# First mixer: query norm folded into the angles, the transposed copies and the exponent; the keys' rotary part turned once; its 64 columns made as rows; other banks and another order of work

## The chip, the cores and the metric

The kernel runs on one core of one Trainium2 chip. The metric is the device time of one execution in microseconds (us); the median of three runs before the change is 1462.47 us (1462.24 to 1466.19). Engines: TensorE (PE: matmuls; PEld: its weight loads), VectorE (DVE), ScalarE (ACT), GpSimd (POOL), and SyncE (SP), which issues the DMAs.

## The reference, cut to what matters

Two transformer blocks on 256 tokens of width 1024, in float32. The change lies in the first block's mixer, mainly in its latent attention:

```python
c_q, c_kv, k_r, hq, hf_f, hf_b, hi, hg = split(rms_norm(x, g_mix) @ w_in)
q  = (rms_norm(c_q,  g_qa)  @ w_qb).reshape(.., 4 heads, 192)      # 128 plain + 64 rotary columns
kv = (rms_norm(c_kv, g_kva) @ w_kvb).reshape(.., 4 heads, 256)     # 128 for k, 128 for v
k  = concat([k_nope, k_r for every head])                          # 128 + 64 shared
q, k = rms_norm(q, g_qn), rms_norm(k, g_kn)                        # over the 192 columns
q, k = [plain part, rope(rotary part, cos, sin)]                   # x1*cos - x2*sin, x1*sin + x2*cos
a  = softmax(q @ k.T * 192**-0.5) @ v
r  = hgrn2(hq, hf_f, hf_b, hi, hg)      # gated linear attention, both directions, chunks of 64
x  = x + concat([a, r]) @ w_o
```

Then a gated feed-forward part, an embedding part (`w_ple_gate`, `w_ple_proj`), and the second block.

## The kernel before

Weights come in 441 units of 128x1024 float32 in the order of a list (`plan`). SP issues unit u's DMA into one of four `raw` buffers once unit u-4 was split. ACT makes the upper half `wh` (`high(n)`: up to unit n), after PE is done with unit u-4; DVE makes the rest `wl` (`low(n)`), and PE waits for it (semaphore `lo`). Each product is three matmuls (upper x upper, upper x lower, lower x upper) into one of eight PSUM banks. `hTh`/`hTl` are the turned, normalised input in two halves, `lTh`/`lTl` the turned latents, `mh`/`ml` the turned mixer output.

Every engine runs one instruction stream in the order in which its function is written, and stops at each `wait_ge`. That hand-written order is what sets the schedule. The unit kinds: `unit_T` gives tokens as rows (two halves q of 128 tokens), `unit_E` gives columns as rows (128 columns by 256 tokens), `unit_D` is a rank-128 update of a 256x1024 sum.

The first mixer's stages on PE: `w_in` 0 to 511 (latents, units 0 to 3); unit 4, the 64 rotary key columns (48 matmuls that move 64 columns each); the forward gates (`gate(0)` to `gate(3)`, `unit_E`) with the latents' transposes behind `gate(1)`; `w_qb` and `w_kvb` (units 9 to 12); `q_part(0..3)`; `heads_turned` (transposes of the plain parts of q or k and of the rotated parts `qr`); the value units (`w_in` 2112), with the keys' `heads_turned` inside; `gate(4)`; `score(0)`, `score(1)`, `inner`, and so on; `hg(0..3)` (`w_in` 2624); the output projection `w_o(0..3)` between the chunk states (`states`) and their outputs (`output`), then its units 4 to 7 by halves; `w_ple_proj`; the feed-forward loop.

On DVE, query and key heads go the same way (lines 708 to 734): mean of squares, root on POOL (`root`, an ALU.pow on 8 columns), eight scalings by root and gain (L717), and the turning by angle (L731, L732, L734), all ahead of PE's transposes. `kr` (the 64 columns) is copied from PSUM at L609 and repeated into `kf` at L611. ACT copies the transposes into `qTn`, `kTn`, `qTr` (L1425); `vt` is copied behind `to_end(0)` (L1541). POOL multiplies the forward `qz` (L443).

## Time and profile before

| | us |
|---|---|
| median of 3 runs | 1462.47 |
| the profiled execution | 1460.53 |
| its span, first to last instruction | 1458.8 |
| PE busy | 1414.6 (97%) |
| DVE busy | 970.9 (67%) |
| ACT busy | 791.7 (54%) |
| POOL busy | 43.2 (3%) |
| mean granted PE clock | 0.990 of full |

The span is cut by instruction spans on each engine; 1.7 us of the execution lie around it. Matmuls overlap in the record, so PE's work is best read from one start to the next. "[idle before <-releaser]" behind a row tells how long the engine stood idle before it and which engine, tile and line ended that.

### The profile page before, as it was taken

How to read it: one execution, taken by the hardware profiler on the slowest of the kernel's cores; microseconds unless marked ns; L12 is line 12 of the kernel's file. 1: busy time of each engine (PE TensorE's matmuls, PEld its weight loads, DVE VectorE, ACT ScalarE, POOL GpSimd, SP SyncE). 2: the span in 40 equal slices, each digit the busy share in tenths (PEclk: the TensorE clock that was granted, in tenths of full speed). 3: DMA queues.
4: the chain of work that ended last, by engine and by line, in shares of the span. 5: the costliest groups of instructions: out<-in, count | busy, mean ns of one | idle time of the engine just before them, and what ended most of it. 6: DMA issues, size and time to landing. Idle time of an engine off the chain costs nothing.

```text
span 1458.8 us, 23164 instructions
## 1 busy us (share of the span) xinstructions
PE 1414.6 (97%) x9070; PEld 1280.6 (88%) x9070; DVE 970.9 (67%) x1738; ACT 791.7 (54%) x1468; POOL 43.2 (3%) x48
## 2 busy tenths in 40 slices
PE   7989999999999999999999999999999999999996
PEld 6878799999787787799999999999998888888885
DVE  6767655555764565768999577778865555555554
ACT  6856444444553554455445677777745455454552
POOL 2211200000000000000000000000000000000000
PEclk9999999999998999999999999999999999999999
DMA  7423365555442345555555544444455656655552
GB/s 251 145 89 136 102 222 185 184 188 179 158 145 98 110 139 171 190 188 170 179 172 165 184 145 144 133 143 146 137 168 189 242 189 194 195 190 199 189 195 79
DMA packets 66925, 241.66 MB, mean 166 GB/s; under 512 B 8192, under 2 KB 8576, under 8 KB 66432
## 3 DMA queue, kind: packets, MB, share of 16 engines
q1 hardware_dynamic: 66816, 240.17, 50.4%
q8 instruction: 73, 1.20, 0.3%
q14 instruction: 36, 0.29, 0.1%
HBM read 238.04 MB, written 2.10 MB: 165 GB/s over the span
## 4 chain that ended last, share of the span: by engine, by line
PE 85%; DVE 10%; ACT 3%; issue 1%; DMA 0%; POOL 0%; SPq 0%; DVEq 0%; POOLq 0%; ACTq 0%
PE bank L2000 83%; DVE wl L523 3%; PE bank L2075 1%; ACT wh L1419 1%; DVE eq L1289 1%; DVE eq L1292 1%; DVE ij L1295 1%; PE bank L2063 1%; DMA x<-in_x 0%; POOL st L439 0%; DVE t L660 0%; DVE e L666 0%; DVE e L669 0%; DVE pos__220 L1226 0%; DVE h L541 0%
## 5 line engine op out<-in xcount | busy, mean ns | idle before, releaser
L523 DVE TENSOR_TENSOR wl<-raw,wh 128x1024 fp32r<-128x1024 f32 x429 | 523.7, 1223 | 292.6 <-ACT wh L1419 292.1
L1419 ACT ACTIVATE wh<-raw 128x1024 fp32r<-128x1024 f32 x429 | 451.2, 1055 | 259.4 <-PE bank L2000 256.9
L2000 PE MATMUL bank<-hTh,wh 128*128 128x256 f32 x1632 | 471.0, 289 | 8.9 <-ACT vt L1425 5.1
L2000 PE MATMUL bank<-hTh,wl 128*128 128x256 f32 x1632 | 464.2, 284 | 0.0
L2000 PE MATMUL bank<-hTl,wh 128*128 128x256 f32 x1632 | 464.0, 284 | 0.0
L2000 PEld LDWEIGHTS bank<-hTh,wh 128*128 128x128 f32 x1632 | 315.6, 193 | 11.8 <-ACT vt L1425 5.5
L2000 PEld LDWEIGHTS bank<-hTl,wh 128*128 128x128 f32 x1632 | 315.5, 193 | 0.8
L2000 PEld LDWEIGHTS bank<-hTh,wl 128*128 128x128 f32 x1632 | 315.0, 193 | 0.0
L2000 PE MATMUL bank<-wh,hTh 128*128 128x512 f32 (+1 forms) x760 | 253.8, 395 | 1.1 <-DVE hTl L549 0.7
L2000 PE MATMUL bank<-wh,hTl 128*128 128x512 f32 (+1 forms) x760 | 249.8, 389 | 0.0
L2000 PE MATMUL bank<-wl,hTh 128*128 128x512 f32 (+1 forms) x760 | 249.7, 389 | 0.0
L2000 PEld LDWEIGHTS bank<-wh,hTh 128*128 128x128 f32 x760 | 143.4, 189 | 31.0 <-issue 1.8
L2000 PEld LDWEIGHTS bank<-wh,hTl 128*128 128x128 f32 x760 | 143.6, 189 | 30.0
L2000 PEld LDWEIGHTS bank<-wl,hTh 128*128 128x128 f32 x760 | 143.9, 189 | 28.5
L1926 ACT ACTIVATE gates<-bank 128x256 f32<-128x256 f32 (+31 forms) x118 | 38.2, 324 | 77.1 <-PE bank L2000 77.1
L2000 PE MATMUL bank<-oi,oj 128*128 128x128 f32 x512 | 67.4, 274 | 0.0
L2000 PEld LDWEIGHTS bank<-oi,oj 128*128 128x128 f32 x512 | 62.7, 192 | 0.0
L1378 DVE TENSOR_TENSOR gates<-bank,gates 128x220 f32<-128x220 f32 (+31 forms) x64 | 32.9, 514 | 38.3 <-ACT gates L1425 38.3
L1924 ACT ACTIVATE ga<-bank 128x256 f32<-128x256 f32 (+32 forms) x73 | 21.0, 288 | 68.5 <-PE bank L2000 68.5
L439 POOL TENSOR_TENSOR st<-st,mhalf 128x1 f32<-128x1 f32 (+2 forms) x15 | 15.3, 1020 | 1333.0 <-DVE st L530 1126.6
L1383 DVE TENSOR_TENSOR hTl<-gates,hTh 128x256 fp32r<-128x256 f32 x126 | 52.5, 417 | 0.0
L1425 ACT ACTIVATE hTh<-gates 128x256 fp32r<-128x256 f32 x126 | 50.3, 400 | 0.0
(361 smaller groups left out, 1300.2 us busy)
## 6 DMA issues: line engine op xcount, KB each, us to landing
raw<-in_wts SPq DMA_DIRECT2D x441, 512.0 KB, 3.5
x<-in_x SPq DMA_DIRECT2D x2, 512.0 KB, 4.6
sk<-in_sk SPq DMA_DIRECT2D x1, 1024.0 KB, 6.4
spill<-x SPq DMA_DIRECT2D x1, 1024.0 KB, 7.9
x<-spill SPq DMA_DIRECT2D x1, 1024.0 KB, 5.6
out<-h SPq DMA_DIRECT2D x2, 512.0 KB, 2.6
gb<-in_g_mix SPq DMA_DIRECT2D x1, 512.0 KB, 4.6
gb<-in_g_ffn SPq DMA_DIRECT2D x1, 512.0 KB, 4.5
```

What stands on the lines that cost most here:

```text
L439: signal(e.tensor_tensor(o, ms, mhalf[:, 0:o.free_size()], ALU.pow), name)
L523: e.tensor_tensor(b[:, :], raw[u % RAW][:, :], a[:, :].bitcast(F), ALU.subtract).then_inc(S("lo"), 1)
L1289: n = own.up(e.tensor_tensor(eq[:, a, :, :, :], bc(paf[:, q, a, :, :], 3, 16), io, ALU.is_equal))
L1292: n = own.up(e.tensor_tensor(eq[:, a, :, :, :], eq[:, a, :, :, :], bc(f4[:, :, a, :], 2, 16), ALU.mult))
L1295: t = e.tensor_reduce(ij[:, a, q, :, :], eq[:, a, :, :, :], AX, ALU.add)
L1378: e.tensor_tensor(g, v[:, NE - 1 - n:NE, :], g, ALU.mult).then_inc(S("G"), 1)
L1383: e.tensor_tensor(b, gates[:, ORDER[n], :], a.bitcast(F), ALU.subtract).then_inc(S("al"), 1)
L1419: e.activation(parts_of(u)[0][:, :], raw[u % RAW][:, :], ACT.Copy).then_inc(S("hi"), 1)
L1425: return e.activation(o, i, ACT.Copy)
L1924: t = e.activation(ga[n % 5][:, 0:c], b[:, 0:c], ACT.Gelu)
L1926: t = e.activation(gates[:, ORDER[n], c:256], b[:, c:256], ACT.Gelu)
L2000: return e.matmul(o, l, r, start=first, stop=last, skip_group_check=True)
```

## The change

What it does, part by part:

- The query norm no longer scales `qf`. The gains of the plain part are applied as a per-partition scale in ACT's copy of the transposes (`gqk` is now 128x2, one column for q and one for k); the gains of the rotary part are multiplied into sine and cosine (`rot`, new DMA `gqkr`); the root itself scales the exponent of the softmax (`st[:, 32..39]`) and the negated maximum.
- The keys' rotary part is turned once (`keys_turned`, 128x64) and then multiplied by the four heads' roots (`kr4`); the plain part takes one 128x1024 product.
- Unit 4 is computed with its weights as the stationary operand (64 rows by 256 tokens), copied to `kt` and turned back by two transposes on PE.
- The first `w_kvb` unit uses banks 6 and 7, the second 2 and 3; the queries' transposes use banks 0 and 1 and stand between the `q_part` units.
- `score(0)`, `score(1)` stand ahead of `gate(4)`; ACT copies `vt` ahead of `to_end(0)`; the squares of the queries come after the copies of `kTn`.
- The forward `qz` product goes from POOL to DVE (`decayed_forward`), with its exponential kept in `hgs`. POOL's fills come earlier.
- `hg(3)` ahead of `inner(1,1)`; `w_o` units 0 to 3 by token halves, with the states' outputs and a transpose between the halves; `w_ple_proj`'s last unit by halves; DVE's and ACT's orders there.

```diff
@@ vector
             e.wait_ge(S("done"), nth("K", "w_in", 512, 64) + 1)
-            for q in range(2):
-                e.tensor_copy(kr[:, q, :], B[2 + q][:, 0:64]).then_inc(S("kr"), 1)
-            e.wait_ge(S("kr"), 2)
-            e.tensor_copy(kf[:, :, :, 128:192], bc(kr[:, :, :], 2, 4)).then_inc(S("kfr"), 1)
+            e.tensor_copy(kt[:, :], B[2][0:64, 0:256]).then_inc(S("krT"), 1)
...
             latent_low(1)
+            e.wait_ge(S("kr_ps"), 1)
+            e.tensor_copy(kr[:, :, :], B[3][:, 0:128].rearrange("p (q c) -> p q c", q=2)).then_inc(S("kr"), 1)
+            e.wait_ge(S("kr"), 1)
+            e.tensor_copy(kf[:, :, :, 128:192], bc(kr[:, :, :], 2, 4)).then_inc(S("kfr"), 1)
...
+            def keys_scaled(n):
+                k8 = kf[:, :, :, 0:128].rearrange("p q h c -> p (q h) c")
+                e.wait_ge(S("rs_1"), 2)
+                e.wait_ge(own.sem, n)
+                e.tensor_tensor(k8, k8, bc(st[:, 40:48], 2, 128), ALU.mult).then_inc(S("scaled"), 1)
+                e.tensor_tensor(kr4[:, :, :, :], bc(rk[:, :, :], 2, 4),
+                                bc(st[:, 40:48].rearrange("p (q h) -> p q h", q=2), 3, 64), ALU.mult).then_inc(S("rope"), 1)
...
             low(13)
+            n_rot = angles_weighted()
+            e.wait_ge(own.sem, n_rot)
+            n_rot = keys_turned()
             low(14)
             scan(0)
+            queries_turned()
             low(15)
             v_out(0)
             low(16)
             v_out(1)
-            headed(qf, 0)
             from_step(0, 31, "t1")
-            scaled(qf, 0)
-            headed(kf, 1)
+            headed(1)
             low(17)
-            turned_by_angle(qf, 0)
+            keys_scaled(n_rot)
             low(18)
-            scaled(kf, 1)
             low(19)
-            turned_by_angle(kf, 1)
             low(20)
             inner(0)
-            low(21)
             rope_out(0)
             rope_out(1)
+            headed(0)
+            low(21)
             from_step(0, 63, "t1b")
             low(22)
+            top_score(0)
+            top_score(1)
             low(23)
             k_decayed(0)
-            top_score(0)
-            top_score(1)
...
             low(25)
+            decayed_forward()
...
             out_mean(0)
+            out_scale(0)
             out_mean(1)
-            out_scale(0)
+            mixed_low(1, 0)
             low(35)
             out_scale(1)
-            mixed_low(1, 0)
@@ scalar
             q_out(0, 512)
+            q_out(1, 256)
+            high(14)
             logs(0)
-            high(14)
-            q_out(1, 256)
+            k_out(0)
             high(15)
-            k_out(0)
...
-            embedded(0)
             turn_high(1, 2)
             turn_high(1, 3)
+            embedded(0)
             embedded(1)
@@ tensor
+            def unit_K(unit, o):
+
+                wh_, wl_ = begin(unit)
+                for k in range(8):
+                    c = two(64, k)
+                    mm(o, wh_[:, c], hTh[:, k, :], k == 0, False)
+                    mm(o, wh_[:, c], hTl[:, k, :], False, False)
+                    t = mm(o, wl_[:, c], hTh[:, k, :], False, k == 7)
+                t.then_inc(S("done"), 1)
...
             gate(0)
+            e.wait_ge(S("krT"), 1)
+            for q in range(2):
+                p = e.transpose(B[3][:, two(64, q)], kt[:, two(128, q)], ident[0:64, 0:64])
+            p.then_inc(S("kr_ps"), 1)
             gate(1)
...
             e.wait_ge(S("t_lo"), 2)
+            unit_T(("T", "w_kvb", 0, 512, 0), B[6:8], lTh, lTl, 2, 512, True, True)
             e.wait_ge(S("qf"), 2)
-            unit_T(("T", "w_kvb", 0, 512, 0), B[2:4], lTh, lTl, 2, 512, True, True)
-            e.wait_ge(S("qf"), 4)
-            unit_T(("T", "w_kvb", 512, 512, 0), B[0:2], lTh, lTl, 2, 512, True, True)
-            for n in range(4):
-                q_part(n)
+            unit_T(("T", "w_kvb", 512, 512, 0), B[2:4], lTh, lTl, 2, 512, True, True)
+            q_part(0)
+            q_part(1)
             heads_turned(qf, 0, 0)
+            q_part(2)
             heads_turned(qf, 0, 1)
-            e.wait_ge(S("va"), 4)
+            q_part(3)
+            e.wait_ge(S("nope"), 2)
+            e.wait_ge(S("ropeT"), 2)
             for k in range(4):
                 unit_T(("T", "w_in", 2112, 512, k), B[0:2], hTh, hTl, 2 * k, 512, k == 0, k == 3)
-                if k == 2:
+                if k == 1:
                     heads_turned(kf, 1, 0)
                     heads_turned(kf, 1, 1)
-            gate(4)
             score(0)
             score(1)
+            gate(4)
             inner(0, 0)
```

Three places show how the rows move. First DVE, around the end of the 64-column unit (`kr` is its copy; `kt` and `krT` are new; `cq` the latents). Before:

```order
L605 COPY cq<-bank 128x512 x2
L523 TENSOR_TENSOR wl_63<-raw_55,wh_59 128x1024
L609 COPY kr<-bank 128x64 x2
L611 COPY kf<-kr 128x8x64
L530 TENSOR_SCALAR st<-st 128x4
L523 TENSOR_TENSOR wl_60<-raw_52,wh_56 128x1024
L618 SCALAR_TENSOR_TENSOR cq<-cq,st,gqa 128x256 x4
```

and DVE at the same place now:

```order
L605 COPY cq<-bank 128x512 x2
L523 TENSOR_TENSOR wl_63<-raw_55,wh_59 128x1024
L608 COPY kt<-bank 64x256
L530 TENSOR_SCALAR st<-st 128x4
L523 TENSOR_TENSOR wl_60<-raw_52,wh_56 128x1024
L615 SCALAR_TENSOR_TENSOR cq<-cq,st,gqa 128x256 x4
```

The two copies of `kr` and the one into `kf` went to behind the latents' lower halves; one copy of `kt` stands in their place, and PE now waits for it between `gate(0)` and `gate(1)`.

Second ACT, from the exponentials of `from_middle(0)` to the second direction's first gate (`vt` the values of the linear attention, `P` the softmax's exponentials). Before:

```order
L1533 ACTIVATE e_107<-t_105 128x1024
L1419 ACTIVATE wh_56<-raw_52 128x1024
L1419 ACTIVATE wh_57<-raw_53 128x1024
L1425 ACTIVATE kTn<-bank 128x4x128 x2
L1419 ACTIVATE wh_58<-raw_54 128x1024
L1541 ACTIVATE e_108<-t_105 128x1024
L1419 ACTIVATE wh_59<-raw_55 128x1024
L1425 ACTIVATE vt<-bank 128x512 x2
L1548 ACTIVATE P,sm<-bank,nm 128x256 x4
```

and ACT at the same place now:

```order
L1574 ACTIVATE e_108<-t_106 128x1024
L1458 ACTIVATE wh_56<-raw_52 128x1024
L1458 ACTIVATE wh_57<-raw_53 128x1024
L1458 ACTIVATE wh_58<-raw_54 128x1024
L1544 ACTIVATE kTn<-bank,gqk 128x4x128 x2
L1534 ACTIVATE sqm,st<-qf 128x192 x8
L1458 ACTIVATE wh_59<-raw_55 128x1024
L1464 ACTIVATE vt<-bank 128x512 x2
L1580 ACTIVATE e_109<-t_106 128x1024
L1587 ACTIVATE P,sm<-bank,nm,st 128x256 x4
```

The copy of `vt` passed the exponential L1541 (now L1580), and the eight squares of the queries came in behind `kTn`.

Third PE, from the last output of the linear attention (`St`, `qz`) to the first units of the second half of `w_o` (`o_` the normalised output, `mh_91` before and `mh_92` now the turned copy of it). Before:

```order
L2000 MATMUL bank<-vt,At 128x128
L2000 MATMUL bank<-St,qz 128x128
L2000 MATMUL bank<-wh_56,mh_90 128x512 x2
L2000 MATMUL bank<-wl_60,mh_90 128x512 x2
L2000 MATMUL bank<-wh_56,ml_92 128x512 x2
L2000 MATMUL bank<-wh_56,mh_90 128x512 x2
L2000 MATMUL bank<-wl_60,mh_90 128x512 x2
L2000 MATMUL bank<-wh_56,ml_92 128x512 x2
L2075 MATMUL bank<-ident,o__99 128x128 x4
L2000 MATMUL bank<-wh_57,mh_91 128x512 x2
```

and PE at the same place now:

```order
L2041 MATMUL bank<-St,qz 128x128
L2041 MATMUL bank<-wh_59,mh_91 128x512 x2
L2041 MATMUL bank<-wl_63,mh_91 128x512 x2
L2041 MATMUL bank<-wh_59,ml_93 128x512 x2
L2041 MATMUL bank<-wh_56,mh_91 128x512 x2
L2041 MATMUL bank<-wl_60,mh_91 128x512 x2
L2041 MATMUL bank<-wh_56,ml_93 128x512 x2
L2124 MATMUL bank<-ident,o__100 128x128 x4
L2041 MATMUL bank<-wh_56,mh_91 128x512 x2
L2041 MATMUL bank<-wl_60,mh_91 128x512 x2
L2041 MATMUL bank<-wh_56,ml_93 128x512 x2
L2041 MATMUL bank<-wh_57,mh_92 128x512 x2
```

The output stands half a unit earlier, and half a unit (three rows) now lies between the transposes of `o_` and the first product that reads them.

## Rows read from the trace of the kernel before

**Rows 1.** The page, part 1: busy time (share of the span) and instructions.

```profile
PE 1414.6 (97%) x9070; PEld 1280.6 (88%) x9070; DVE 970.9 (67%) x1738; ACT 791.7 (54%) x1468; POOL 43.2 (3%) x48
```

**Rows 2.** PE's waits from 0 to 260 us: in total, times, longest.

```profile
PE bank L2000 <- ACT vt L1425: 5.1, 1, 5.1
PE bank L2000 <- DVE ml L774: 2.0, 1, 2.0
PE bank L2122 <- DVE qr L734: 1.8, 1, 1.8
PE bank L2000 <- ACT hgs L1645: 1.1, 1, 1.1
PE bank L2000 <- DVE hTl L549: 1.1, 1, 1.1
PE bank L2000 <- ACT qf L1425: 0.8, 1, 0.8
```

**Rows 3.** Windows: us, then busy (x) of PE, PEld, DVE, ACT, POOL; PEclk, DMA share, GB/s.

```profile
12.31:23.53 11.22, 11.22 (x48) 9.04 (x49) 9.40 (x25) 7.46 (x10) 0.38 (x3) 1.00 0.72 232
23.53:28.81 5.28, 5.28 (x50) 5.28 (x48) 3.98 (x7) 2.49 (x10) 0.00 (x0) 1.00 0.66 206
28.81:36.15 7.34, 7.34 (x51) 7.34 (x51) 5.51 (x11) 4.40 (x5) 4.21 (x3) 0.77 0.60 191
36.94:42.76 5.82, 5.82 (x51) 5.82 (x49) 5.79 (x7) 3.10 (x6) 1.94 (x2) 1.00 0.54 177
42.76:54.65 11.89, 10.32 (x50) 8.21 (x49) 7.29 (x10) 8.68 (x13) 0.00 (x0) 1.00 0.53 162
60.00:80.00 20.00, 18.25 (x118) 16.35 (x117) 18.25 (x36) 17.88 (x40) 9.27 (x4) 1.00 0.34 119
87.00:91.38 4.38, 4.38 (x24) 4.38 (x25) 1.78 (x2) 0.36 (x1) 0.00 (x0) 0.62 0.60 226
```

**Rows 4.** DVE in order of time, 24 to 37 us: start, us, what [idle before].

```profile
29.70 1.23 DVE L523 TENSOR_TENSOR wl<-raw,wh 128x1024 fp32r<-128x1024 f32 x1 [2.12 <-ACT wh L1419]
30.84 0.35 DVE L609 COPY kr<-bank 128x64 f32<-128x64 f32 x2
...
33.77 1.67 DVE L618 SCALAR_TENSOR_TENSOR cq<-cq,st,gqa 128x256 f32<-128x256 f32 x4 [0.91 <-POOL st L439]
```

**Rows 5.** All engines in order of time, 83 to 88 us.

```profile
84.39 1.06 ACT L1541 ACTIVATE e<-t 128x1024 f32<-128x1024 f32 x1 [3.91 <-DVE t L660]
...
86.30 1.06 ACT L1425 ACTIVATE vt<-bank 128x512 f32<-128x512 f32 x2
...
86.93 0.58 PE L2000 MATMUL bank<-hTh,wh 128*128 128x256 f32 x1 [5.06 <-ACT vt L1425]
```

**Rows 6.** POOL in order of time, 30 to 130 us.

```profile
59.56 2.55 POOL L439 TENSOR_TENSOR st<-st,mhalf 128x8 f32<-128x8 f32 x1 [20.60 <-DVE st L530]
65.03 3.21 POOL L439 TENSOR_TENSOR st<-st,mhalf 128x8 f32<-128x8 f32 x1 [2.92 <-DVE st L530]
75.98 4.30 POOL L443 TENSOR_TENSOR qz<-e,qT 128x512 f32<-128x512 f32 x2 [7.74 <-DVE qr L734]
```

**Rows 7.** DVE's groups by line, 55 to 84 us: xcount | busy us, mean ns.

```profile
L666 DVE TENSOR_TENSOR e<-e,qT 128x1024 f32<-128x1024 f32 x1 | 2.3, 2314 | 0.0
```

**Rows 8.** DVE in order of time, 124 to 130 us.

```profile
126.84 1.23 DVE L666 TENSOR_TENSOR e<-e,qT 128x1024 f32<-128x1024 f32 x1 [0.80 <-ACT e L1532]
```

**Rows 9.** DVE in order of time, 106 to 111.5 us.

```profile
108.11 0.66 DVE L762 COPY PT<-bank 128x512 f32<-128x512 f32 x1
110.92 1.23 DVE L523 TENSOR_TENSOR wl<-raw,wh 128x1024 fp32r<-128x1024 f32 x1 [2.15 <-ACT wh L1419]
```

**Rows 10.** DVE in order of time, 146 to 160 us.

```profile
147.40 0.73 DVE L700 SCALAR_TENSOR_TENSOR St<-St,dl,bank 128x128 f32<-128x128 f32 x2
```

**Rows 11.** PE in order of time, 149 to 149.4 us.

```profile
149.26 0.38 PE L2000 MATMUL bank<-vt,At 128*128 128x128 f32 x2
```

**Rows 12.** ACT in order of time, 174 to 184 us.

```profile
180.31 3.92 ACT L1419 ACTIVATE wh<-raw 128x1024 fp32r<-128x1024 f32 x4
```

More of the change, by code:

```diff
@@ L1503, in nope_out @@
                 e.wait_ge(S("nope_ps"), 2 * i + q + 1)
-                copy((qTn, kTn)[i][:, :, 128 * q:128 * q + 128],
-                     B[(2, 6)[q]][:, :].rearrange("p (h t) -> p h t", h=4)).then_inc(S("nope"), 1)
+                e.wait_ge(S("in_small"), 112)
+                e.activation((qTn, kTn)[i][:, :, 128 * q:128 * q + 128],
+                             B[(2, 6)[q] if i else 0][:, :].rearrange("p (h t) -> p h t", h=4), ACT.Copy,
+                             scale=gqk[:, i:i + 1]).then_inc(S("nope"), 1)
             def rope_out(q):
@@ L1525, in decays @@
                              ACT.Exp).then_inc(S("dl"), 1)
[L1526 removed]
+                e.activation(e3b[:, :] if d else hgs[:, :, :].rearrange("p q c -> p (q c)"), b, ACT.Exp).then_inc(S("eb"), 1)
             def from_middle(d):
@@ new lines, in unit_K, with part_D @@
+            def unit_K(unit, o):
[6 more added lines that the diff above has]
+                t.then_inc(S("done"), 1)
+            def part_D(held, xh, xl, base, q, first, last):
+                s = two(128, q)
+                for a, b, f, z in ((xh, held[0], first, False), (xh, held[1], False, False), (xl, held[0], False, last)):
+                    for n in range(2):
+                        t = mm(B[base + 2 * q + n][:, :], a[:, s], b[:, two(512, n)], f, z)
+                return t
@@ L2048, in unit_D @@
             def unit_D(unit, xh, xl, base, first, last, half=False):
-                wh_, wl_ = begin(unit)
+                held = begin(unit)
                 for q in range(2):
-                    s = two(128, q)
-                    for a, b, f, z in ((xh, wh_, first, False), (xh, wl_, False, False), (xl, wh_, False, last)):
-                        for n in range(2):
-                            t = mm(B[base + 2 * q + n][:, :], a[:, s], b[:, two(512, n)], f, z)
+                    t = part_D(held, xh, xl, base, q, first, last)
```

251 lines of the change are left out of this document (139 added, 112 removed).

## The prediction

> **What bounds the kernel now.** I read the page's totals first. TensorE (PE) is busy 97% of a span of 1458.8 us [rows 1], so the end moves only if PE does less work, works at its higher clock for longer, or waits less. The change touches only the first block's mixer and the start of its feed-forward part, that is the first 183 us, so next comes who PE waits for there [rows 2]. The largest wait after the start is 5.1 us on a copy of `vt` by ScalarE (ACT). The others are 2.0 us on `ml`, 1.8 us on `qr`, 1.1 us each on `hgs` and `hTl`, and 0.8 us on the copy of `qf`. The windows then cut PE's row at the places that the change touches [rows 3]. They show two stretches where PE never idles and is slow all the same. From 28.81 to 36.15 the granted clock averages 0.77, and from 87.00 to 91.38 it averages 0.62: part of each runs at 1.2 GHz instead of 2.4. The first stretch follows the 5.28 us of the 64-column unit, the second follows the 5.1 us wait.
>
> **The change part by part.** Unit times are taken from start to start. One weight unit of 24 matmuls (128x256) at full clock takes 5.82/2 = 2.91 us [rows 3] (window 36.94:42.76).
>
> *The 64-column unit.* Before: 48 matmuls in 5.28 us, 110 ns each [rows 3]. After: 24 matmuls whose output is 64 rows by 256 columns. No row shows that form. The nearest is the 2.91 us unit, equal but for 128 output rows, and I take 2.9. The bounds are 24 x 110 ns = 2.6 us and 5.0 us, if the form ran at half clock. Gain 2.4 us.
> The trace shows 110 ns for a matmul that moves only 64 columns; a weight load of 128 columns stands beside each. The Trainium skill (TensorE: Matmul & The Clock Gate, "LDWEIGHTS (loading the stationary operand)") says that a weight load's time follows its columns, P/1.2 ns: about 107 ns for 128 columns and 53 for 64. By that page the new form is paced by its 256 moving columns, about 109 ns each (same page, "Back-to-back issue gap"), and the unit would be 2.6 us, 0.3 better than in my sum.
>
> *The clock behind it.* Two units ran in 7.34 us where 5.82 is full clock [rows 3]. With a full-rate moving operand in place of the 5.28 us of narrow matmuls I expect no drop there: gain 1.5. Bounds: 0 and 1.5.
>
> *The new wait.* `kr` used to be copied by VectorE (DVE) and nothing waited for it soon. Now PE, right behind `gate(0)`, must transpose `kt`, and DVE's copy of `kt` still stands behind the same `wl` (29.70) in DVE's queue, which itself waited for ACT [rows 4]. PE reaches the transposes at 23.53 + 2.9 + 2.91 = 29.3. The copy starts at 30.84 as before and takes 0.22 (one `kr` copy) to 0.42 (a 128x256 copy); I take 0.40, so it is done at 31.25. That is a wait of 1.9 us plus 0.25 for two transposes (bounds 0.1 and 0.6). Behind it `gate(1)` and everything on PE is queued. `gate(1)` ends at 34.4. The scaled latents then come 0.4 earlier than the row at 33.77, as DVE has less to copy; the fourth is ready at 35.1, so `latents(1)` adds 0.3. Loss 2.45 us. The first block up to w_qb thus gains only 2.4 + 1.5 - 2.45 = 1.45: it starts at 41.3 instead of 42.76.
>
> *w_qb and w_kvb.* 11.89 us with 10.32 busy [rows 3], so two gaps of 0.8 us. The first w_kvb unit goes to banks 6 and 7 and waits for no copy of `qf`, and the logarithm with its table load now stands behind both `q_out` on ACT. Both 0.8 us waits go; start to start this is 2.0 us, as the matmuls' overlap comes back too: 36 matmuls of 512 columns at 0.234 (11.22/48, window 12.31:23.53) and 12 of 256 at 0.121 make 9.9 against 11.89. Gain 2.0, bounds 1.5 and 2.1.
>
> *Queries and keys.* Queries now need no root, no scaling and no mean ahead of the rotation: `rope` is done when six DVE operations of 0.41 to 0.43 us follow the scan, at about 55, and PE asks for it at 57.7. The 1.8 us wait for `qr` goes: gain 1.75. What is late next is ACT's `nope`/`rope_out` of half 0, which PE asks for after `q_part(2)`, at 60.6. ACT's queue up to it (k_out, two `wh`, k_out, eight squares, a table load, `silu`, `wh`, `silu`, copies) sums to 60.4: 0.2 us spare. If it is late, PE pays that lateness one for one. A root of 8 columns on POOL took 2.55 and 3.21 us [rows 6]; with 3.2 the scaled keys are there at 65.0 and PE asks at 69.7. The queries' root is asked for only by the scores' maxima: done at 79.1, asked at 80.0.
>
> *DVE.* Sixteen scalings, two groups of 8 at 2.7 us each, become one 128x1024 product (1.2) and one 128x512 (0.7); the keys' six turning operations shrink to 128x64, with four small ones for the weighted angles. POOL no longer multiplies `qz` from 75.98 to 80.28 [rows 6], while DVE's product took 2.31 us [rows 7] against 1.23 for the same line with POOL idle [rows 8]: 2.2 us of DVE back for the two products. Added are two products for `qz`, 1.4 us, behind `low(25)`, ahead of the copy of `PT` at 108.11. They fit in the 2.15 us of idle that follows it [rows 9]; the copy ends at 110.2 where PE asked at 110.4. I take 0, bound 0.5 lost.
> The Trainium skill (GPSIMD Engine Reference, "Key points") says that GpSimd shares its SBUF interfaces with VectorE and contends with DVE instructions of two SBUF inputs. The 2.31 against 1.23 agrees.
>
> *The wait for vt.* Before, PE idled for 5.06 us up to 86.93 since ACT's copy of `vt` was queued behind an exponential that waited for DVE [rows 5]. After, the copy stands ahead of that exponential, and the scores stand ahead of `gate(4)`. By my walk PE ends the value units at 76.5; `kTn` and `kTr` are there by 74.2, `vt` at 77.2, and `gate(4)` wants it at 80.0. Gain 5.1, and with the idle goes the half clock behind it: 24 matmuls in 4.4 us at a granted 0.62 [rows 3] against 2.91, gain 1.5. Next late: the first probabilities, ready at 81.7, asked at 86.6. Bounds: 2 (if the root of the queries, behind eight squares, is the new end) and 6.6.
> The trace grants 0.62 right after that idle time. The Trainium skill (TensorE: Matmul & The Clock Gate, "What's actually happening") says that the half clock is the default and that activity releases it. By that page the new 1.9 us wait could bring half clock behind it, which would add 1.5 us to my sum; in the trace the 1.8 us wait for `qr` brought none (it lies in the window 60:80, with 1.00).
>
> *98.6 to 138.* Same work, shifted. Moving `hg(3)` ahead of `inner(1,1)` does not help: the 1.1 us wait for `hgs` ended on ACT's own queue. 0.
>
> *Output projection.* `output(1,*)` now starts half a `w_o` unit, 1.43 us, earlier than 149.26 (at 147.83), but needs the last `St`, done at 148.13 [rows 10, 11]: with the signal 0.4 of wait. `t_lo` for the second half no longer stands behind `low(35)` and a second `out_scale`, and half a unit covers the transposes' copies. The 2.0 us wait becomes 0.1 to 0.2 us; with the `St` wait inside the 1.43 already counted, the net is 2.0 - 0.4 = 1.6. Bounds 0.5 and 2.0.
>
> *ple_proj.* The last transposes come before half a unit, so the 1.1 us wait for `hTl` shrinks to 0.4. But `low(40)` still waits for ACT's `wh` at 180.31, behind four `pp` copies [rows 12]; that moves only 0.3. Net 0.3.
>
> Sum: 1.45 + 2.0 + 1.75 + 5.1 + 1.5 + 1.6 + 0.3 = 13.7 us. The profiled execution took 1460.53 us (span 1458.8 and 1.7 around it); 1460.53 - 13.7 = 1446.8. The runs' median is 1462.47, 1.9 above that execution, so I give 1448.8. From 183 us to the end PE is the bound, with the same instructions.
>
> **Rivals.**
> (1) *The waits gather elsewhere.* With slacks of 0.2 us at ACT's `rope_out` and the stall for `kt`, one or two more stalls of 1 to 2 us appear, and the clock drops after the `kt` wait (1.5 us lost as at 28.81). 13.7 - 4.5 = 9.2, or 1453.3. For it: ACT is busy 17.9 of the 20 us from 60 to 80 [rows 3]. Against: the later slacks are 2 to 5 us.
> (2) *The vt wait is only renamed.* Eight query squares and a root now stand between the `kTn` copies and the maxima; the chain has 86.6 - 81.7 = 4.9 us to spare. Were it 10 us later than I have it, PE would idle 5 us at `score(2)` and pay the half clock behind that once more: 1448.8 + 6.6 = 1455.4. Against: squares and root are 2.8 and 3.2 us, all counted.
> (3) *Nothing reaches the end*: a stage behind is paced by something else (the weights' DMA). Against: PE's row names no such wait [rows 2], and the DMA share is 0.34 in the window 60:80. 1462.
> (4) *Slower: the clock.* One mechanism: behind the `kt` wait at 29.3 the clock falls to 1.2 GHz and does not come back as it did within the 7.34 us window. Every us of PE's full-clock work then takes two. It decides from 13.7 us of such work on; all of it up to the end of w_kvb at 51.2 is 20 us and would give 1448.8 + 20 = 1468.8. Against: both drops in rows 3 ended inside their windows (means of 0.77 and 0.62, not 0.50), with PE busy.
>
> **How the numbers follow.** Forecast 0.62, (1) 0.2, (2) 0.1, (3) 0.05, (4) 0.03. 0.3% is 4.4 us, about what a measurement can tell from no change: faster means below 1458.1. Faster 0.91, same 0.06, slower 0.03. The range reaches 3 us down (terms at their better bounds, and the 1.9 us by which a median run may stand less apart from the profiled one) and up to between (1) and (2): 1445.5 to 1454.5.
>
> **What would show it.** Right: the 64-row unit in 2.6 to 2.9 us; a PE wait of about 1.9 us on the copy of `kt`; granted clock 1.00 from 23 to 100 us; no wait on `vt`, `qr`, `qf`; every PE row behind 183 us some 13.7 us earlier. Wrong: a PE wait over 2 us on `P`, `kTn`, `qTr` or `nm`; a clock drop behind the `kt` wait; DVE's `e` products still at 2.3 us; an `ml` wait that stays at 2.0.

## The result, and the profile after

The changed kernel took 1446.97 us (median of four runs, 1439.0 to 1449.7) against 1464.33 us for the kernel before on the same chip: ratio 0.9869, 95% interval 0.9821 to 0.9917. On another chip six runs gave 1446.79 and 0.9871 (0.9843 to 0.99). The direction was right. (The ratios are formed from the single runs; the medians alone stand at 0.9881 and 0.9886.) The gain was larger than forecast: 0.9869 of the 1462.47 us on which the forecast stood is 1443.3 us, and the range ended at 1445.5. The forecast itself was a ratio of 0.9907. The first interval still holds it and the second does not, so it takes the second comparison to show that the gain is larger. The median of 1446.97 us by itself lies inside the stated range; it is against the kernel before, measured beside it, that the gain is larger than the range allows.

The profiled execution of the changed kernel took 1439.0 us (span 1437.3, mean clock 0.997). PE's waits from 0 to 260 us (in total, times, longest) answer to [rows 2]:

```profile
PE bank L2112 <- DVE h L541: 7.9, 2, 7.5
PE bank L2041 <- DVE wl L523: 2.3, 3, 1.1
PE bank L2302 <- DVE kt L608: 1.6, 1, 1.6
PE bank L2041 <- DVE hTl L549: 0.5, 1, 0.5
PE bank L2041 <- DVE St L701: 0.3, 1, 0.3
```

The waits for `vt`, `ml`, `qr`, `qf` and `hgs` are gone; the one for `kt` is there, and three of 0.4 to 1.1 us for `wl`. (The 7.5 us on `h` is the start of the kernel, which the change leaves alone.) The windows answer to [rows 3]; the columns are the same:

```profile
23.89:26.61 2.72, 2.72 (x25) 2.72 (x24) 2.69 (x4) 0.31 (x1) 0.00 (x0) 1.00 0.41 124
31.55:41.33 9.78, 9.78 (x82) 9.58 (x81) 8.76 (x16) 5.31 (x8) 2.01 (x2) 1.00 0.71 213
41.33:51.16 9.83, 9.83 (x51) 8.21 (x50) 8.02 (x19) 8.09 (x13) 0.00 (x0) 1.00 0.52 167
60.00:80.00 20.00, 20.00 (x113) 17.47 (x113) 13.44 (x15) 18.57 (x38) 5.07 (x2) 1.00 0.46 153
24.00:170.00 146.00, 141.67 (x933) 127.69 (x932) 110.23 (x177) 101.95 (x193) 24.13 (x19) 1.00 0.41 134
```

The first row is the 64-row unit: 2.72 us for 24 matmuls. The third is w_qb and w_kvb, with no gap. The fourth is busy for all of its 20 us where before it had 18.25. The last says that from 24 us on the whole mixer ran at 2.4 GHz. DVE's row at the `kt` copy, the answer to [rows 4]:

```profile
29.68 1.23 DVE L523 TENSOR_TENSOR wl<-raw,wh 128x1024 fp32r<-128x1024 f32 x1 [2.13 <-ACT wh L1458]
30.83 0.41 DVE L608 COPY kt<-bank 64x256 f32<-64x256 f32 x1
...
33.36 0.48 DVE L615 SCALAR_TENSOR_TENSOR cq<-cq,st,gqa 128x256 f32<-128x256 f32 x1 [0.92 <-POOL st L447]
```

And ACT around the `vt` copies, the answer to [rows 5]:

```profile
76.65 1.06 ACT L1464 ACTIVATE vt<-bank 128x512 f32<-128x512 f32 x2
78.31 1.06 ACT L1580 ACTIVATE e<-t 128x1024 f32<-128x1024 f32 x1 [0.60 <-DVE t L661]
```

The copies now end before the exponential starts, and PE never asks for them in vain.

A ruler for all runs below: the time from the first matmul of the first T unit to the first matmul of the feed-forward's down projection (the first PE row with `ah`). It leaves out the start, whose length differs from one execution to the next, but not all of the slow clock that each execution begins with. The views give 1.00 there, because the record of the clock only begins when it first comes up; the matmuls show it. The same two microseconds of the T units hold 9 matmuls in the first profile of the kernel before, whose clock record begins at 11.80, and 6 in the second, whose record begins at 16.29:

```profile
14.00:16.00 2.00, 2.00 (x9) 1.42 (x8) 2.00 (x3) 0.64 (x2) 0.00 (x0) 1.00 0.51 205
```
```profile
14.00:16.00 2.00, 2.00 (x6) 1.57 (x5) 2.00 (x3) 0.57 (x1) 0.00 (x0) 1.00 0.55 219
```

The ruler's far end in the two profiles, before and after:

```profile
191.89 0.39 PE L2000 MATMUL bank<-wh,ah 128*128 128x512 f32 x1
```
```profile
178.01 0.39 PE L2041 MATMUL bank<-wh,ah 128*128 128x512 f32 x1
```

The first T units start at 12.31 and 12.28 us, so the ruler reads 179.58 before and 165.73 after: 13.85 us gained, where the sum said 13.7. The two spans differ by 7.6 us more than this (1458.8 - 1437.3 = 21.5). Between 431 and 558 us the one profile has three stretches of half clock, 17.1 us long, and the other has none; half of 17.1 is 8.5, some of it spent in waits. (Both have one more at the very end, from 1452.2 and 1430.0 us on, which costs 3.3 and 3.6.) Below, "lost" is half the length of such a stretch; what it costs PE is less where PE waits inside it. How much of such half clock a kernel has is what the experiments had to settle.

### The profile page after: what moved, and what is told of

Its sections match the earlier page's. It is cut to its first block, busy times and chain, and to the rows that moved or that the text cites. A ratio compares the mean times of both kernels' runs of the same rounds, so it can differ in the third digit from the quotient of the medians.

```text
span 1437.3 us, 23117 instructions
## 1 busy us (share of the span) xinstructions
PE 1401.6 (98%) x9048; PEld 1269.7 (88%) x9048; DVE 966.8 (67%) x1730; ACT 792.4 (55%) x1468; POOL 39.3 (3%) x46
## 4 chain that ended last, share of the span: by engine, by line
PE 85%; DVE 10%; ACT 3%; issue 1%; DMA 0%; POOL 0%; SPq 0%; DVEq 0%; POOLq 0%; ACTq 0%
PE bank L2041 83%; DVE wl L523 3%; PE bank L2124 1%; ACT wh L1458 1%; DVE eq L1328 1%; DVE eq L1331 1%; DVE ij L1334 1%; PE bank L2112 1%; DMA x<-in_x 0%; DVE St L701 0%; ACT kdz L1464 0%; DVE hTl L549 0%; DVE pos__225 L1265 0%; DVE h L541 0%; DVE x L1002 0%
## 5 line engine op out<-in xcount | busy, mean ns | idle before, releaser
L2041 PE MATMUL bank<-hTh,wh 128*128 128x256 f32 (+1 forms) x1640 | 471.2, 287 | 3.9 <-DVE wl L523 3.3
L2041 PE MATMUL bank<-hTh,wl 128*128 128x256 f32 (+1 forms) x1640 | 464.5, 283 | 0.0
L2041 PE MATMUL bank<-hTl,wh 128*128 128x256 f32 (+1 forms) x1640 | 464.3, 283 | 0.0
L2041 PEld LDWEIGHTS bank<-hTh,wh 128*128 128x128 f32 (+1 forms) x1640 | 314.2, 192 | 6.6 <-issue 2.3
L2041 PEld LDWEIGHTS bank<-hTl,wh 128*128 128x128 f32 (+1 forms) x1640 | 314.2, 192 | 0.9
L2041 PEld LDWEIGHTS bank<-hTh,wl 128*128 128x128 f32 (+1 forms) x1640 | 313.8, 191 | 0.0
L2041 PE MATMUL bank<-wh,hTh 128*128 128x512 f32 x744 | 248.0, 395 | 1.1 <-DVE hTl L549 0.7
L2041 PE MATMUL bank<-wh,hTl 128*128 128x512 f32 x744 | 244.3, 390 | 0.0
L2041 PE MATMUL bank<-wl,hTh 128*128 128x512 f32 x744 | 244.0, 390 | 0.0
L2041 PEld LDWEIGHTS bank<-wl,hTh 128*128 128x128 f32 x744 | 140.0, 188 | 28.1
L1967 ACT ACTIVATE gates<-bank 128x256 f32<-128x256 f32 (+31 forms) x118 | 38.2, 324 | 76.5 <-PE bank L2041 76.5
```

Source lines behind the costliest of these rows:

```text
L1967: t = e.activation(gates[:, ORDER[n], c:256], b[:, c:256], ACT.Gelu)
L2041: return e.matmul(o, l, r, start=first, stop=last, skip_group_check=True)
```

## The experiments

**The changed kernel again** (no edit; timed).

> The changed kernel once more, nothing altered. The first look gave 1446.97 us against 1464.33 (ratio 0.9869), but the four runs of it spread over 10.7 us (1439.0 to 1449.7) with granted clocks of 0.989 to 0.997. Theory A: the program itself is 13.9 us shorter up to the row that starts at 169.27 us (183.15 before), of which 3.4 us is half clock that is gone in the mixer, and all the rest of the spread is half-clock stretches of 3.4 us in the later blocks that come and go: span times granted clock is then 1433 us within 1 in every run (1443.6 for the run before), and the median span about 1445 with a mean clock near 0.991. Rival B: the profiled run's missing later drops belong to the change: then most runs have a clock near 0.997 and spans near 1438.

Measured: spans from 1437.6 to 1447.0 and clocks from 0.990 to 0.998; two of the six runs had 0.998, four had 0.990 to 0.993. Span times clock is 1432.5 to 1435.2 in all of them (1432.0 to 1433.2 in the first four). For the kernel before it is 1441.9 to 1444.6 over the 11 runs beside it, at clocks of 0.984 to 0.990. Theory A holds, with 2.2 us for its 1: the products' means differ by 10.1 us, which is the program, and the rest, 6 to 7 of the medians' 17 us, is clock. (The clock is given to three places, so a product is good to 0.7 us, and it does not see the slow clock of the start.) In the means the clock's part is larger, since span less product is 19.4 us on average for the kernel before and 9.4 for the changed one.

**More profiles of both kernels.** No edit.

> The kernel before, looked at once more, for where its half clock lies. The profile that the prediction used had 3.4 us behind the 64-column unit and 3.4 behind the wait for vt (3.4 us lost in the mixer, 3.0 counted). Theory A: that was the light case; one or both stretches are 6.8 us here, as in two other kernels with the 64-column unit, so 5 to 7 us are lost in the mixer, and the later places (behind the scores of the second block and v2a's wait) lose 5 to 10. Rival B: 3.4 and 3.4 again, and what the runs have beyond the forecast lies in the later blocks alone.

> The kernel before, a third look. Theory A: a stretch behind the 64-column unit (from 28 to 30 us) and one behind the wait for vt (from 87 to 88), each 3.4 or 6.8 us long, in every execution; the mixer loses 3.4 to 8.5 us. Rival B: one of them is missing in some executions.

> The changed kernel, a third look. Theory A: no half clock between 23 and 170 us again; any that there is lies from 415 us on, behind the second block's scores or behind v2a's wait. Rival B: half clock behind the kt wait of 1.64 us (31.6) in some executions, as one other kernel had it behind a kt wait of 2.0 us.

> The changed kernel, a fourth look, for the same question: Theory A no half clock between 23 and 170 us, Rival B a stretch of 3.4 us from 32 us on.

Half-clock windows of the kernel before, in its second profile and then in its third:

```profile
29.94:36.77 6.83, 6.83 (x34) 6.83 (x34) 4.83 (x10) 1.20 (x2) 4.33 (x4) 0.50 0.48 167
87.97:94.80 6.83, 4.58 (x21) 4.58 (x22) 3.11 (x3) 2.68 (x4) 0.00 (x0) 0.50 0.56 188
163.06:166.48 3.42, 3.42 (x9) 2.65 (x10) 0.98 (x1) 0.00 (x0) 0.00 (x0) 0.50 0.64 235
```
```profile
28.50:35.33 6.83, 6.83 (x34) 6.83 (x34) 4.13 (x9) 3.16 (x8) 2.10 (x3) 0.50 0.52 177
89.94:93.36 3.42, 3.29 (x15) 3.29 (x16) 1.98 (x2) 0.56 (x2) 0.00 (x0) 0.50 0.75 277
```

In the profile of the forecast these were 3.4 and 3.4 us. The third stretch of the second profile stands right behind PE's wait of 2.0 us for `ml`, ahead of the second half of `w_o`:

```profile
162.96 1.15 PE L2000 MATMUL bank<-wh,mh 128*128 128x512 f32 x2 [2.01 <-DVE ml L774]
```

The changed kernel had none between 24 and 170 us in any of four profiles. The window in the third:

```profile
24.00:170.00 146.00, 142.64 (x934) 128.25 (x932) 109.92 (x179) 102.13 (x194) 24.16 (x19) 1.00 0.39 135
```

| profile | ruler, before | half clock in it from 24 us on | ruler, after | half clock in it from 24 us on |
|---|---|---|---|---|
| first | 179.58 | 3.4 + 3.4 | 165.73 | none |
| second | 184.76 | 6.8 + 6.8 + 3.4 | 165.77 | none |
| third | 181.76 | 6.8 + 3.4 | 165.80 | none |
| fourth | | | 165.72 | none |

The change gained 13.85 us against the profile that the forecast read, but 16.0 and 19.0 against the others. The additions, 2.2 and 5.2 us, are the longer half clock of the mixer (1.7 and 5.1 lost beyond the first profile's 3.4) and 0.8 and 1.9 us lost in the T units, less what fell into waits: the longer stretch behind the wait for `vt` has PE busy for only 4.58 of its 6.83 us. The changed kernel also has up to 2.9 us of half clock in its T units, but there it shortens the wait for `kt` (0.9 us in the third and fourth profile instead of 1.64) and costs next to nothing. Theory A holds in all four, though the second profile of the kernel before lost more in the mixer (8.5 for 5 to 7) and later (12.0 for 5 to 10) than it allowed. From 415 us on, up to the stretch at the very end, both kernels have it: the changed one in two profiles of four (8.5 us lost in each), the one before in all three (8.5, 12.0 and 8.5). Behind the second block's scores and the 2.15 us wait in front of `PT` (its turned probabilities) PE ran 17 to 24 us at 1.2 GHz where there was any, 8.5 to 12 us lost. That is about the 10 us by which runs of one kernel differ.

**The old 64-column unit in the changed kernel.**

```diff
-            unit_K(("K", "w_in", 512, 64), B[2][0:64, 0:256])
+            unit_K_old(("K", "w_in", 512, 64), B[2:4])
...
-            e.tensor_copy(kt[:, :], B[2][0:64, 0:256]).then_inc(S("krT"), 1)
+            for q in range(2):
+                e.tensor_copy(kr[:, q, :], B[2 + q][:, 0:64]).then_inc(S("kr"), 1)
```

> The changed kernel with the 64-column unit as it was: 48 matmuls of 64 columns, output 128x64 in two banks, kr copied straight from them, no kt and no transposes; all other parts of the change stay. Theory A (terms 1 to 3 of the sum, and narrow matmuls lower the clock behind them): unit 5.28 us instead of 2.72, then a half-clock stretch of 3.4 us that starts near 28.9 (1.7 us lost), no wait of 1.64 and no transposes: w_qb starts at 42.7 to 42.9 instead of 41.33, and the row of 169.27 at 170.7 to 170.9. Rival B (the drop had another cause, for one the early start of the clock): no half-clock stretch, w_qb at 41.2, nothing lost. Rival C: two 64-column units' worth of drop, as the unit now meets full clock later: more than one stretch of half clock.

> The changed kernel with the old 64-column unit, timed now. Its first look had half clock from 29.44 to 36.27 us, 6.8 us long where the kernel before had 3.4, and with the half clock taken out (half of 6.83 and of the first microseconds) its way from the first T unit to w_qb was 28.3 us against 28.45 in the changed kernel: the shorter unit and the new kt wait cancel, and only the clock is left. Theory A: span times granted clock is 1433 as in the changed kernel, and the median is 1.7 to 3.4 us above its 1446.9, near 1449.5, by lower clocks alone. Rival B: the later blocks' half clock outweighs it and the median is within 1 us of 1446.9.

The half clock is back behind the unit, with PE never idle ahead of it, and twice as long as theory A of the first run had it (6.83 us, rival C's size). The unit's window and the one behind it, first profile:

```profile
24.89:30.17 5.28, 5.28 (x46) 5.28 (x45) 3.16 (x5) 2.65 (x9) 0.00 (x0) 0.93 0.62 199
29.44:36.27 6.83, 6.83 (x33) 6.83 (x33) 4.90 (x10) 1.17 (x2) 1.26 (x2) 0.50 0.50 176
```

The ruler reads 170.21 and, in the timed kernel's profile, 169.46: 4.5 and 3.7 us more than the changed kernel, 3.4 of it the half clock. Of the rest, some is half clock in the T units, which run into the `kt` wait in the changed kernel and are hidden there. So the shorter unit pays only by the clock; the wait for `kt` eats the 2.6 us that it is shorter by. But timed, the kernel takes 1445.82 us (ratio 0.9868, 0.9847 to 0.9889), 1 us less than the changed kernel, which by the intervals is no difference. Rival B of the timed run was right: span times clock is 1433.9 to 1434.9, and its clocks are 0.992 to 0.994 in all six runs, where the changed kernel's are 0.990 to 0.993 in four and 0.998 in two. It has half clock in the mixer and, in the timed runs, less of it later: in the timed kernel's profile one stretch, from 536.6 to 543.5 us. (The first profile had three later ones, 17.1 us long; no run shows what decides.) A stretch won in one place was not won in the kernel's time.

**The vt copies back** in the changed kernel, with `gate(4)` ahead of the scores.

```diff
+            to_end(0)
             high(23)
             e.wait_ge(S("done"), nth("T", "w_in", 2112, 512, 3) + 1)
             for q in range(2):
                 copy(vt[:, q, :], B[q][:, :]).then_inc(S("v"), 1)
-            to_end(0)
...
+            gate(4)
             score(0)
             score(1)
-            gate(4)
```

> The changed kernel with ScalarE's copies of vt behind the exponential of to_end(0) and one wh again, and gate(4) ahead of the scores. VectorE makes t at 78.28, so the exponential ends at 79.3, wh at 80.4, the first vt at 81.0; PE ends the value units at 76.4 and idles 4.6 us. Theory A (term 7): 4.6 us and a half-clock stretch of 3.4 us behind the idle (1.7 us): the row of 169.27 comes at 175.6 (6.3 later). Rival B: the idle brings no half clock (or the clock falls for other reasons): 4.6 later, 173.9. Rival C: the delay is taken back later, because the next waits (1.1 us at w_o, 0.3 at St, 0.5 at hTl) have other ends: less than 3 us later.

PE's row at `gate(4)`, and the half-clock window behind it:

```profile
81.57 0.38 PE L2041 MATMUL bank<-hTh,wh 128*128 128x256 f32 x1 [4.36 <-ACT vt L1464]
```
```profile
81.83:85.24 3.41, 3.41 (x18) 3.41 (x18) 0.00 (x0) 0.18 (x1) 0.00 (x0) 0.50 0.24 94
```

From w_qb to the down projection it takes 142.8 us instead of 136.7: 6.1 lost, 4.4 of wait and 1.7 of clock. Theory A, to 0.2 us.

**The vt copies moved and nothing else**, in the kernel before (the same three lines, the other way round).

> The kernel before with one edit: ScalarE's two copies of vt ahead of the exponential of to_end(0). Nothing else of the change. PE ends the value units at 81.9, the copies end at 82.5 and 83.1, gate(4) can start at 82.6 where it stood at 86.9. Theory A (term 7 can be had alone): wait 0.7 instead of 5.1 us, no half clock behind it (1.5), so the down projection's first row (191.89) 5 to 6 us earlier. Rival B: ScalarE's exponential still comes at 85.4, k_decayed and the probabilities with it, and PE meets them as a new wait at the products of kd or at the second scores: 2 to 3 us gained. Rival C: half clock stays, since it follows the scores as much as the idle time: 1.7 us less gained than in A.

> The kernel before with the vt copies alone moved ahead of to_end(0), timed. Its first look: 5.8 us less from w_qb to the down projection, no half clock behind it, no later half clock either, 1449.3 us. Theory A: span times clock falls by 4.1 to 4.3 (the 5.1 us wait less the 0.7 and 0.8 that are left, 1443.6 to 1440), the clock rises by one or two stretches of 3.4 us, and the median is 6 to 8 us under the kernel before, near 1457. Rival B: the first look's absence of later half clock belongs to the edit: median near 1450.

From w_qb to the down projection it takes 143.3 us where before took 149.1: 5.8 gained, with no half clock at the place. The wait for `vt` fell from 5.06 to 0.73 us. (The 0.8 us that the expectation counts beside it stands in front of the first `w_kvb` unit, in the kernel before too, and has nothing to do with the edit.) Timed it gives 1458.38 us, ratio 0.9949 (0.9929 to 0.9969), and span times clock of 1439.6 to 1441.4, on average 3.2 us less than the kernel before, where 4.1 to 4.3 were expected. Theory A in kind, a little short in both: the median is 5.6 us lower, for 6 to 8, by one moved line. The first profile, without later half clock (1449.3 us), was the exception. The timed kernel's profile has 3.4 us of half clock from 156.7 on, 1.4 us behind the end of the 2.0 us wait for `ml`: the same place as in the second profile of the kernel before.

**The wait filled** in the kernel before.

```diff
+            for _ in range(40):
+                mm(B[4][:, 0:256], hTh[:, 0, 0:128], hTh[:, 0, :], True, True)
             gate(4)
```

> The kernel before with 40 matmuls of 256 columns that compute nothing used, put in front of gate(4), where PE idles 5.06 us for vt. They take about 4.85 us at 121 ns each, so PE waits 0.2 us instead. Theory A (the idle time brings the half clock): granted clock 1.00 from 82 to 98 us, and gate(4) and the scores behind it run 1.7 us (or 3.4) faster, though not one us of the wait itself is gained. Rival B (the rows around it, transposes and 64-column keys, bring it): half clock from 87 to 88 us all the same, nothing gained.

Windows of the 40 matmuls and of `gate(4)`:

```profile
85.63:90.60 4.97, 4.95 (x41) 4.74 (x39) 3.97 (x6) 2.31 (x3) 0.00 (x0) 1.00 0.39 122
90.83:93.81 2.98, 2.98 (x25) 2.98 (x26) 1.86 (x2) 0.44 (x1) 0.00 (x0) 1.00 0.78 286
```

`gate(4)` takes 2.98 us at full clock where [rows 3] have 4.38 at 0.62. From w_qb to the down projection it takes 147.7 us, 1.5 less than the kernel before in its best profile. Theory A: the idle time brought the half clock, in three profiles of three of the kernel before and in the run with the `vt` copies back; in this one profile, work that nobody uses takes it away. This is as the Trainium skill (TensorE: Matmul & The Clock Gate, "What's actually happening") has it, that activity releases the half clock. Behind the 64-column unit idle time is not needed: all eight profiles of kernels that hold the old unit have half clock behind it, with PE busy throughout.

**Where the kt wait goes.** First the `kt` copy alone is moved:

```diff
+            e.wait_ge(S("done"), nth("K", "w_in", 512, 64) + 1)
+            e.tensor_copy(kt[:, :], B[2][0:64, 0:256]).then_inc(S("krT"), 1)
             low(7)
-            e.wait_ge(S("done"), nth("K", "w_in", 512, 64) + 1)
-            e.tensor_copy(kt[:, :], B[2][0:64, 0:256]).then_inc(S("krT"), 1)
```

> VectorE's copy of kt ahead of the wl that it waited behind; nothing else moved. K is done at 26.6, so the copy ends near 27.9 instead of 31.24 and PE's wait of 1.64 us in front of the transposes goes. Theory A (the wait was worth what the prediction charged): w_qb starts 1.6 us earlier, at 39.7, and so does everything up to the row of 169.27 us. Rival B (renamed): the mean of the squares still stands behind wl, POOL's root and the scaled latents come at 34.2 (two of them) and 35.0 (four) less 0.3, while PE now reaches the latents' transposes at 32.7: a wait of 1.2 to 1.5 us on cq takes its place and the gain is 0.3 us. Rival C: the kt wait had kept the clock up or its end lets it fall: granted clock below 1.00 somewhere between 23 and 45 us.

PE's waits from 24 to 60 us with the copy alone moved:

```profile
PE bank L2150 <- DVE cq L615: 0.9, 1, 0.9
```

With a second, shorter one of 0.14 us right behind it this took the place of the 1.64. Gain on the ruler 0.3 to 0.4 us: rival B.

Then the mean goes with it, and the four scalings ahead of the next `low`:

```diff
+            mean(st[:, 40:44], st[:, 6:10], "sq_1", 4, 256, "ms_1")
             low(7)
-            mean(st[:, 40:44], st[:, 6:10], "sq_1", 4, 256, "ms_1")
-            low(8)
             e.wait_ge(S("rs_1"), 1)
...
+            low(8)
```

> VectorE's copy of kt and the mean of the squares ahead of wl, and the four scalings of the latents ahead of the next wl. With the copy of kt alone moved the wait became one of 0.93 and 0.14 us for cq, and only 0.4 us was gained. Theory A: the mean now comes at 28.5 (squares done 28.4 on ScalarE), POOL's root is there by 30.6, the scalings run from 30.9 to 32.6 and PE, which reaches the latents' transposes at 32.7, waits for none of kt and cq: counted from the start of the 64-row unit, w_qb comes at 15.6 to 15.9 us instead of 17.45 (17.06 with kt alone), and the down projection's first row (178.01 us in the changed kernel) 1.5 to 1.9 us earlier, at 152.2 to 152.6 from that start instead of 154.13. Rival B: a third wait takes their place, on ScalarE's lTh or VectorE's lTl or kr in front of w_qb: under 1 us gained.

DVE in order of time:

```profile
28.34 0.42 DVE L607 COPY kt<-bank 64x256 f32<-64x256 f32 x1 [0.62 <-PE bank L2041]
28.89 0.17 DVE L530 TENSOR_SCALAR st<-st 128x4 f32<-128x4 f32 x1
29.84 1.23 DVE L523 TENSOR_TENSOR wl<-raw,wh 128x1024 fp32r<-128x1024 f32 x1 [0.78 <-ACT wh L1458]
30.98 1.67 DVE L614 SCALAR_TENSOR_TENSOR cq<-cq,st,gqa 128x256 f32<-128x256 f32 x4
```

PE then waits for nothing between 24 and 60 us; w_qb comes 15.55 us behind the unit's start instead of 17.45, and the down projection 152.25 instead of 154.13. Theory A. On the ruler it is 165.20, only 0.5 less than the changed kernel: this execution began with 4.2 us of half clock in its T units (2.1 us lost), which the changed kernel hides in its `kt` wait and this one cannot.

**The old order of the output projection** in the changed kernel (`w_o` units whole, the small steps between them; DVE's `out_scale` and `mixed_low` as before).

```diff
             for k in range(4):
                 held = begin(("D", "w_o", k))
                 w_o(k, 0, held)
-                if k == 2:
-                    output(1, 0)
-                    output(1, 1)
-                elif k == 3:
-                    mixed(1, 0)
                 w_o(k, 1, held)
+                ...
```

> The changed kernel with the output projection as before: states, output(1,*) and mixed(1,0) between whole w_o units, and VectorE's out_scale(0) behind the second mean with mixed_low behind out_scale(1). Theory A (term 9, 1.6 us): the wait of about 2.0 us on ml comes back, the St wait of 0.27 goes, and the down projection's first row comes 1.6 to 1.8 us later than 154.13 from the start of the 64-row unit. Rival B: with all the rest earlier the wait on ml is hidden by what VectorE has free, and it is under 0.5 us later. Rival C: half clock behind the wait adds 1.7.

Two of PE's waits between 24 and 160 us:

```profile
PE bank L2041 <- DVE ml L800: 2.0, 1, 2.0
PE bank L2302 <- DVE kt L608: 2.0, 1, 2.0
```

From `w_o(0)` to the down projection it takes 53.7 us instead of 52.2 (unrounded, 1.45 more). Theory A in kind, with 1.45 for 1.6; counted from the 64-row unit the row comes 3.1 us later, and the other 1.7 are rival C's, though not behind the wait that it named. This execution also shows what the prediction's rival 4 spoke of, at the size of one stretch: behind its `kt` wait of 2.0 us stands this window:

```profile
31.80:35.21 3.41, 3.41 (x17) 3.41 (x17) 2.49 (x6) 1.48 (x2) 1.81 (x2) 0.50 0.84 241
```

That is 1.7 us lost. The changed kernel, with 1.64 us of wait or less, had it in none of its four profiles. The wait for `ml` that the old order brings had half clock behind it in two of the seven profiles that hold it (the stretches at 163.1 and 156.7 us above), not in this one.

**The later waits covered** in the changed kernel, in the second block.

```diff
             query(1, "v2b", 2)
-            score2(0)
             query(2, "rb", 1)
+            score2(0)
             query(3, "f_dve", 2)
-            score2(1)
             proj(0, 0, 2, "kqb", 4)
+            score2(1)
...
-            gate_out(2)
             late_probs(7)
+            gate_out(2)
```

> The changed kernel with three waits of the second block covered: query(2) ahead of score2(0), proj(0,0) ahead of score2(1) (VectorE's qb_out(2) and qb_out(3) moved with them), and VectorE's late_probs(7) ahead of gate_out(2). Here all later half-clock stretches began: behind the waits of 0.95, 0.95 and 2.15 us on PE. Theory A (a stretch needs idle time and slow rows together): the 4.05 us of waits go and no run has half clock in these places: mean clock 0.997 in every run, times near 1435, median 12 us under the changed kernel's 1446.9. Rival B (the score rows alone, with 8 rows of cc by sel and 128 columns, lower the clock): 4.0 us gained, the clocks spread from 0.989 to 0.997 as before, median near 1443. Rival C (the waits move): under 2 us gained.

The waits went (none is left on `qzb`, the second block's queries, or on `PT`), and the half clock stayed, shorter. Windows of its profile, behind each of the two groups of scores:

```profile
421.00:425.00 4.00, 4.00 (x22) 3.90 (x21) 1.55 (x3) 1.72 (x9) 0.00 (x0) 0.57 0.01 2
431.60:435.20 3.60, 3.60 (x12) 3.01 (x12) 2.67 (x4) 2.49 (x10) 0.00 (x0) 0.53 0.18 69
```

PE is busy without a pause before both, with the score rows of 128 columns, so idle time is not needed here (rival B's cause). The next kernel's profile has three stretches, from 429.2, 439.4 and 456.5 us on, and PE has no wait in it between 400 and 470. But without the waits the clock is 0.994 to 0.996 in all four runs and they lie within 3.5 us instead of 9 to 11. Median 1438.25, ratio 0.9818 (0.9794 to 0.9843): 8.6 us under the changed kernel, 4 of them the waits. That lies between theory A's 12 us and rival B's 4; span times clock is 1428.0 to 1428.9, about 5 us lower, and the rest is clock.

**The orders together**: e_kt_mean's, e_later's, and `branch_low(1, 0)` and `branch_low(0, 0)` (DVE's lower halves `bTl`, for which PE waited 0.8 and 1.5 us in the second block) each ahead of one `low`.

```diff
-            low(u0 + 28)
             branch_low(0, 0)
+            low(u0 + 28)
```

> The changed kernel with the orders that the runs point to: kt, mean and scalings early (the row of the down projection 1.9 us earlier), the second block's scores and late_probs covered (4.05 us of waits gone), and in addition VectorE's branch_low(1,0) and branch_low(0,0) each ahead of one wl, for the two waits of 0.8 and 1.5 us on bTl. Theory A (each wait gone is gone to the end, since PE is the bound): span times clock 1433 less 1.9, 4.05 and 2.3, so 1424.8; median 1430 to 1433, ratio to before near 0.978. Rival B: bTl's wait is renamed as wl's, and 2.3 of it stay: 1432 to 1436.

Measured: 1432.79 us (1431.99 to 1435.45), ratio 0.9775 (0.9753 to 0.9798). Span times clock is 1423.8 to 1425.5, and the profile has no wait on `bTl`: theory A. It beats both kernels, the changed one by some 14 us.

## Why the prediction was right on the program and short on the clock

*The 64-column unit.* 2.72 us, for my 2.9. The prediction also drew on two rules of the Trainium skill (TensorE: Matmul & The Clock Gate, "LDWEIGHTS (loading the stationary operand)" and "Back-to-back issue gap"), by which the unit is paced by its 256 moving columns and takes 2.6 us; the trace lies between.

*The new wait.* 1.64 for 1.9; w_qb started at 41.33 for 41.3. What this term left out is that the wait also swallows half clock in the T units ahead of it.

*w_qb and w_kvb.* 9.83 for 9.9. *Queries and keys.* No wait; `qTr` of half 0 ended at 60.38 for 60.4. *DVE.* L667 took 1.22 us instead of [rows 7]'s 2.31 once POOL was idle, as forecast from [rows 8].

*The wait for vt.* PE ended the value units at 76.36 (76.5), `gate(4)` started at 79.63 (80.0), `score(2)` at 86.45 (86.6). Its price was tested both ways: 6.1 and 5.8 us for 6.6.

*98.6 to 138.* The 1.1 us wait stayed, as said, but is now put down to `wl`: the last `hgs` was done at 125.67 and that `wl` at 125.68, so both were late. *Output projection and ple_proj.* 1.5 for 1.9 (the `hTl` wait 0.5 for 0.4, and 0.7 for `wl` behind it).

Against the profile that it read, the gain was 13.85 us for 13.7. By stretches: up to w_qb 1.4 for 1.45, from there to `w_o(0)` 10.9 for 10.35, from `w_o(0)` to the down projection 1.5 for 1.9. The closeness of the sum owes something to luck, since these partly cancel. Without the clock, terms of 10.7 us stand against 10.1 between the means of span times clock.

What failed is the price of the clock: the sum had 3.0 us for it, and the means of the runs differ by 10.0 (19.4 lost before, 9.4 after). **The step that failed is *The clock behind it***, "Gain 1.5. Bounds: 0 and 1.5", and with it the 1.5 us of half clock in *The wait for vt*. Both took the length that one execution showed as the most that can be there. Behind the 64-column unit two profiles of three have 6.8 us of half clock, 3.4 us lost; behind the wait for `vt` one of three has 6.8; and one has another 3.4 behind the wait for `ml`, for which *Output projection* had no clock at all. In the mixer the kernel before lost 3.4, 8.5 and 5.1 us in its three profiles, 5.7 on average. The forecast's own profile was at the light end: no run of the kernel before has a clock above its 0.990, and most have 0.984 to 0.988.

**A second step failed with it, and by the profiles it is the larger part**: the sum put the later blocks at nothing, "From 183 us to the end PE is the bound, with the same instructions". The instructions are the same, but between 200 and 1400 us they lost 8.5, 12.0 and 8.5 us by half clock in the profiles of the kernel before and 0, 0, 8.5 and 8.5 in those of the changed one, so 5.4 us less on average over few profiles. The profile that the forecast stands on has 8.5 us of it, which the prediction does not mention. The range had 3 us for all of this.

Why the changed kernel loses less there stays open. With the old 64-column unit put back the changed kernel again lost 3.4 us in the mixer and still took no longer than without it, since less was lost later. So for the 64-column unit no timed run shows that the half clock won behind it reaches the end, and no run says why a later stretch does or does not come in a given execution.

## What to carry to other kernels

Read the granted clock over the whole span before a sum is made: a stretch at half clock that one profile shows may be twice as long in the next, so its price is a spread and not a number. Span times mean clock tells what of a difference is the program, here to 1 or 2 us. A wait that is taken away is gained on the stretch itself with the half clock behind it (6.1 and 5.8 us here), but a wait in a queue of copies is often only the first of a row of lateness; the next one (here `cq` behind `kt`) is found on the same engine's row. An engine that waits hides lateness ahead of it, so an edit's worth depends on what it lays bare.

## What was not expected of the hardware

PE fell to 1.2 GHz behind 5.28 us of matmuls that move 64 columns, without a pause, in eight profiles of eight, for 3.4 or 6.8 us; in the second block it also fell behind score matmuls of 128 columns whose waits were gone. Behind a wait of 2.0 us the clock fell in some profiles (one of one for `kt`, two of seven for `ml`) and not in others. 40 useless matmuls in a 5 us wait kept it at 2.4 GHz. The full clock after the start came between 11.3 and 17.0 us in different executions of nearly the same program. A copy on ACT with a scale from a column took 0.67 to 0.69 us for 128x512 where the plain one of the same size took 0.58 to 0.60.
